# Merge, value products and output projection of the sample rows in the four column groups of TensorE

## What is computed

```python
def sample_attention(q_lat, q_pe, ckv_new, kr_new, cache_ckv, cache_kr, page_table):
    ...
    carry, _ = lax.scan(page_step, init, page_table.T)      # running max m, sum l, acc over the past rows
    sc_new = jnp.where(causal, scores(ckv_new, kr_new), NEG_INF)
    _, l, acc = update(carry, sc_new, ckv_new)
    o = acc / l[..., None]                                   # 8 sequences x 16 heads x 256 latents
    ...
def mla_out(o_lat, w_ukv, w_o):
    o = jnp.einsum("blhc,chd->blhd", o_lat, w_ukv[..., QK_NOPE:])     # 16 heads x 64
    return o.reshape(o.shape[0], o.shape[1], N_HEADS * V_HEAD) @ w_o  # 1024 x 1024
...
        x = x + ga1[:, None, :] * y
        h = modulate(rmsnorm(x, g_norm[layer, 1]), sh2, sc2)
        x = x + ga2[:, None, :] * peer(h, ...)
```

## Time and profile before

| | us |
|---|---|
| median of 3 runs (3669.32 to 3676.19) | 3672.77 |
| the profiled execution | 3665.84 |
| its span in the trace | 3664.0 |
| busy PE / DVE / ACT / POOL | 2650.3 / 2367.8 / 1223.5 / 1307.2 |
| expert gathers of layer 0 / layer 1, about | 454 to 1790 / 2304 to 3640 |
| attention between them, about | 1930 to 2262 |

### The profile page before, as it was taken

One profiled execution on the slowest core, in us unless ns is written; L12 is line 12 of the kernel. 1 busy time (PEld: TensorE's weight loads), 2 busy tenths in 40 slices (PEclk: granted clock), 3 DMA queues, 4 the chain that ended last, 5 costly groups with the idle time before them and its releaser, 6 DMA issues.

```text
span 3664.0 us, 63101 instructions
## 1 busy us (share of the span) xinstructions
PE 2650.3 (72%) x24936; PEld 987.7 (27%) x24936; DVE 2367.8 (65%) x5633; ACT 1223.5 (33%) x3811; POOL 1307.2 (36%) x1153
## 2 busy tenths in 40 slices
PE   4564899867766866658789996777686668666676
PEld 3353632403200400012225664322031004001100
DVE  8645387687776677555553541878867766765645
ACT  1212133434333333334432220343343343333333
POOL 5300033444444444433413510334444444443432
PEclk7666899867766966769999997777787679777667
DMA  8755599999999999999962044899999999999997
GB/s 330 209 140 200 220 396 411 405 419 410 409 420 419 409 420 420 403 420 381 393 218 107 19 187 157 322 400 403 421 402 417 421 419 409 421 420 400 417 420 319
DMA packets 214367, 1276.43 MB, mean 348 GB/s; under 512 B 54568, under 2 KB 60080, under 8 KB 67208
## 3 DMA queue, kind: packets, MB, share of 16 engines
q0 software_dynamic: 151552, 1109.46, 74.2%
q1 hardware_dynamic: 61968, 162.67, 12.8%
q10 hardware_dynamic: 576, 0.59, 0.1%
HBM read 1258.85 MB, written 11.43 MB: 347 GB/s over the span
## 4 chain that ended last, share of the span: by engine, by line
DMA 35%; PE 35%; DVE 19%; ACT 5%; issue 4%; SPq 1%; DVEq 1%; POOL 0%; PEldq 0%; ACTq 0%; POOLq 0%
DMA arena<-peer_uv,arena 34%; PE psum L2522 12%; DVE arena L1981 8%; PE psum L2469 6%; PE psum L2430 3%; DVE arena L1598 3%; PE psum L2870 2%; PE psum L2601 1%; PE psum L2670 1%; DVE arena L1607 1%; ACT arena L1339 1%; ACT arena L1336 1%; DVE arena L1892 1%; DVE arena L1992 1%; ACT arena L1326 1%
## 5 line engine op out<-in xcount | busy, mean ns | idle before, releaser
L2522 PE MATMUL psum<-arena 32*32 32x512 f32 x16384 | 1528.0, 819 | 740.3 <-ACT arena L1339 733.7
L1101 POOL DMA_INDIRECT arena<-peer_uv,arena x1040 | 1136.4, 1093 | 2007.5 <-PE psum L2522 1536.6
L1981 DVE SCALAR_TENSOR_TENSOR arena<-arena 128x1024 f32<-128x1024 f32 x1040 | 1273.6, 1226 | 743.5 <-DMA arena<-peer_uv,arena 731.7
L2522 PEld LDWEIGHTS psum<-arena 32*32 32x32 f32 x16384 | 216.5, 119 | 1915.0 <-ACT arena L1339 1813.8
L1326 ACT ACTIVATE arena<-arena 128x1 f32<-128x1 f32 x1040 | 210.3, 202 | 1533.3 <-DVE arena L1981 1532.2
L1339 ACT ACTIVATE arena<-arena 128x32 f32<-128x32 f32 x1024 | 329.0, 321 | 33.4
L1336 ACT ACTIVATE arena<-arena 128x1 f32<-128x1 f32 x1040 | 306.0, 294 | 33.8
L2469 PEld LDWEIGHTS psum<-arena 128*128 128x128 f32 x2048 | 245.7, 198 | 72.5 <-issue 69.5
L2469 PE MATMUL psum<-arena 128*128 128x128 f32 x2048 | 263.4, 286 | 2.2 <-ACT arena L1279 2.2
L2327 PE MATMUL psum<-arena 128*9 128x128 f32 x2048 | 98.8, 374 | 111.3 <-DMA arena<-b_mod 111.3
L1598 DVE TENSOR_TENSOR arena<-arena 128x512 f32<-128x512 f32 (+8 forms) x182 | 149.7, 823 | 18.7 <-ACT arena L1169 5.6
(11 more groups left out here) (293 smaller groups left out, 2379.5 us busy)
## 6 DMA issues: line engine op xcount, KB each, us to landing
arena<-w_mod SPq DMA_DIRECT2D x64, 1024.0 KB
arena<-peer_wq SPq DMA_DIRECT2D x12, 2048.0 KB, 12.6
arena<-peer_uv,arena POOLq DMA_INDIRECT x1040, 10.4
arena<-w_glu SPq DMA_DIRECT2D x5, 2048.0 KB, 12.8
arena<-mod_rows SPq DMA_DIRECT2D x4, 1024.0 KB
arena<-w_o SPq DMA_DIRECT2D x1, 4096.0 KB
arena<-x_after_layer SPq DMA_DIRECT2D x7, 512.0 KB
arena<-w_uq SPq DMA_DIRECT2D x1, 3072.0 KB, 15.0
```

The costliest lines, as they stand in the source:

```text
L1101: pool.indirect_dma_start(ring[r], None, a[f"peer_uv{t // 5}"], bass.IndirectOffsetOnAxis(ap=ix, axis=0)).then_inc(landed[r], 16)
L1981: dve.scalar_tensor_tensor(out=u, in0=u, scalar=1.0, in1=h, op0=ALU.mult, op1=ALU.mult, accum_out=at(DOTS + (t % 2) * 2 * P + m, 1)).then_ ...
L2522: ins = pe.matmul(acc_of(t, i, c), diag[rows, r, :], ring[r][rows, D + 512 * c:D + 512 * (c + 1)], start=(m == 0), stop=last, skip_group_c ...
```

## The change

The same results are computed with the work spread over the four column groups.

- `SW` has 32 columns for each sequence and lies where `SNEW` was. In the merge `SW` (32 columns) and `WNM` (16) are now stationary and `acc` and `KVR[0]` (256 latents) move; the sequences 4 r + g, g = 0 to 3, write the four groups of PSUM bank 2, once for r = 0 and once for r = 1. 16 matmuls. The result has heads on partitions and latents in columns, so DVE copies it (128 x 512), PE turns it (4 full turns), and DVE copies it in two parts to `olt`.
- The value products stay 32 matmuls of 64 columns, but heads 4 g + m write group g, so DVE copies 128 x 256 and PE turns 2 pieces.
- The projection writes quarter g of the 1024 outputs to group g: 32 matmuls of 256 columns (`sample_project`).
- Gate and residual rows of the sample are loaded in quarters, 256 columns on partitions 32 g to 32 g + 7, by four DMAs each instead of one; the store is four DMAs too, and the semaphore counts follow.

```diff
@@ program
-        SW = o; o += NB * NH
+        SW = SNEW
@@ attention_sync
-                sp.dma_start(at(MH + D, D, 0, NB), mod_dram[1:NC9, 8 * D:9 * D]).then_inc(s_mw, 16)
+                for g in range(4):
+                    sp.dma_start(at(MH + D, 256, 32 * g, 32 * g + NB),
+                                 mod_dram[1:NC9, 8 * D + 256 * g:8 * D + 256 * (g + 1)]).then_inc(s_mw, 16)
...
+                        for g in range(4):
+                            sp.dma_start(at(MX, 256, 32 * g, 32 * g + NB), x2s_dram[:, 256 * g:256 * (g + 1)]
+                                         ).then_inc(s_rld[0], 16)
@@ attention_store
+                for g in range(4):
+                    sp.dma_start(x3s_dram[:, 256 * g:256 * (g + 1)], at(MX, 256, 32 * g, 32 * g + NB)
+                                 ).then_inc(s_rst[0], 16)
@@ merge (DVE)
-                dve.tensor_tensor(at(SW, NB * NH).rearrange("p (b h) -> p b h", b=NB),
-                                  psum[:, 5, 0:NB].unsqueeze(2).to_broadcast([P, NB, NH]),
-                                  at(EYE, NH).unsqueeze(1).to_broadcast([P, NB, NH]), ALU.mult).then_inc(s_mg, 1)
+                dve.tensor_tensor(at(SW, NB * 32).rearrange("p (b h) -> p b h", b=NB),
+                                  psum[:, 1, 0:NB].unsqueeze(2).to_broadcast([P, NB, 32]),
+                                  eye32.unsqueeze(1).to_broadcast([P, NB, 32]), ALU.mult).then_inc(s_mg, 1)
                 dve.wait_ge(s_mg, 7)
-                dve.tensor_copy(olt, psum[:, 4, 0:2 * NB * NH].rearrange("p (c b h) -> p c h b", c=2, b=NB)
-                                ).then_inc(s_mg, 1)
+                dve.tensor_copy(at(OO, 512), psum[:, 2, :]).then_inc(s_mg, 1)
+                dve.wait_ge(s_mg, 9)
+                for c in range(2):
+                    ins = dve.tensor_copy(olt[:, c].rearrange("p h (r g) -> p h r g", r=2),
+                                          psum[:, 3, :].rearrange("p (r c g h) -> p c h r g", r=2, c=2, g=4)[:, c, 0:NH])
...
@@ attention_pe
-                for c in range(2):
-                    for b in range(NB):
-                        out = psum[:, 4, (c * NB + b) * NH:(c * NB + b + 1) * NH]
-                        pe.matmul(out, acc[:, b, P * c:P * (c + 1)], at(SW + b * NH, NH), start=True, stop=False)
-                        ins = pe.matmul(out, at(KVR[0] + P * c, P, 0, NB), at(WNM + b * NH, NH, 0, NB),
-                                        start=False, stop=True)
+                for r in range(2):
+                    for g in range(4):
+                        b = 4 * r + g
+                        pe.matmul(psum[32 * g:32 * g + 32, 2, KVL * r:KVL * (r + 1)], at(SW + b * 32, 32), acc[:, b, :],
+                                  start=True, stop=False, skip_group_check=True)
+                    for g in range(4):
+                        b = 4 * r + g
+                        ins = pe.matmul(psum[32 * g:32 * g + NH, 2, KVL * r:KVL * (r + 1)],
+                                        at(WNM + b * NH, NH, 0, NB), at(KVR[0], KVL, 0, NB), start=False, stop=True,
+                                        skip_group_check=True)
                 ins.then_inc(s_mg, 1)
                 pe.wait_ge(s_mg, 8)
-                for h in range(NH):
-                    for c in range(2):
-                        ins = pe.matmul(psum[0:NB, h // 8, VH * (h % 8):VH * (h % 8 + 1)], olt[:, c, h, :],
-                                        wv[:, c, VH * h:VH * (h + 1)], start=(c == 0), stop=(c == 1))
+                for j in range(4):
+                    ins = pe.transpose(psum[:, 3, P * j:P * (j + 1)], at(OO + P * j, P), ident)
+                ins.then_inc(s_mg, 1)
+                pe.wait_ge(s_mg, 10)
+                for m in range(4):
+                    for c in range(2):
+                        for g in range(4):
+                            h = 4 * g + m
+                            ins = pe.matmul(psum[32 * g:32 * g + NB, 0, VH * m:VH * (m + 1)], olt[:, c, h, :],
+                                            wv[:, c, VH * h:VH * (h + 1)], start=(c == 0), stop=(c == 1),
+                                            skip_group_check=True)
                 ins.then_inc(s_os, 1)
-                project(4)
+                sample_project()
@@
+            def sample_project():
+
+                pe.wait_ge(s_on, 1)
+                for j in range(2):
+                    ins = pe.transpose(psum[:, 1, P * j:P * (j + 1)], at(OO + 512 + P * j, P), ident)
+                ins.then_inc(s_ot, 1)
+                pe.wait_ge(s_otc, 9)
+                ot = at(OTT, D).rearrange("p (k t) -> p k t", k=KD)
+                for k in range(KD):
+                    for g in range(4):
+                        ins = pe.matmul(psum[32 * g:32 * g + NB, 2, 0:256], ot[:, k, 0:NB],
+                                        wo[:, k, 256 * g:256 * (g + 1)], start=(k == 0), stop=(k == KD - 1),
+                                        skip_group_check=True)
+                ins.then_inc(s_yy, 1)
```

More of the change, by code:

```diff
@@ L242, in row_no @@
                     if row_slot(q, m) == slot and not (passes is LOADS and (q, m) in NOT_LOADED)]
-            return 16 * len(mine)
+            return 16 * sum(4 if row == ("residual", 4) else 1 for row in mine)
         ROUNDS = ([("u", r) for r in range(NR)] + [("k", r) for r in range(NR)]
@@ L1560, in attention_act @@
                 act.wait_ge(s_ot, 1)
-                act.activation(at(OTT, D).rearrange("p (k t) -> p k t", k=KD)[:, :, 0:NB],
-                               psum[:, 6:8, :].rearrange("p b (k t) -> p (b k) t", k=4)[:, :, 0:NB], ACT.Copy
+                act.activation(at(OTT, D).rearrange("p (g j t) -> p j g t", g=4, j=2)[:, :, :, 0:NB],
+                               psum[:, 1, 0:256].rearrange("p (j g t) -> p j g t", j=2, g=4)[:, :, :, 0:NB], ACT.Copy
                                ).then_inc(s_otc, 1)
@@ L2240, in attention_dve @@
                 dve.wait_ge(s_os, 1)
[L2241 removed]
+                dve.tensor_copy(at(OO + 512, 256), psum[:, 0, 0:256]).then_inc(s_on, 1)
                 attention_out(4)
@@ L2272, in merge @@
                 dve.wait_ge(s_mg, 1)
-                nmt, lmt = psum[0:NB, 4, 0:P], psum[0:NB, 4, P:2 * P]
+                nmt, lmt = psum[0:NB, 0, 0:P], psum[0:NB, 0, P:2 * P]
                 link(dve.tensor_reduce(mn, nmt.rearrange("p (g h) -> p h g", g=4), AX.X, ALU.min))
@@ L2780, in attention_pe @@
                 pe.wait_ge(s_cnm, NB)
-                pe.transpose(psum[0:NB, 4, 0:P], at(NM, NB), ident)
-                pe.transpose(psum[0:NB, 4, P:2 * P], at(LSUM, NB), ident).then_inc(s_mg, 1)
+                pe.transpose(psum[0:NB, 0, 0:P], at(NM, NB), ident)
+                pe.transpose(psum[0:NB, 0, P:2 * P], at(LSUM, NB), ident).then_inc(s_mg, 1)
                 pe.wait_ge(s_mg, 4)
-                pe.transpose(psum[:, 5, 0:NB], at(EX, P, 0, NB), ident[0:NB, 0:NB]).then_inc(s_mg, 1)
+                pe.transpose(psum[:, 1, 0:NB], at(EX, P, 0, NB), ident[0:NB, 0:NB]).then_inc(s_mg, 1)
@@ L2853, in project @@
             def project(j):
-                R = rows5(j)
-                if j == 4:
-                    pe.wait_ge(s_on, 1)
-                    for k in range(KD):
-                        ins = pe.transpose(psum[:, 6 + k // 4, P * (k % 4):P * (k % 4) + R], at(OO + P * k, P, 0, R),
-                                           ident[0:R, 0:R])
-                    ins.then_inc(s_ot, 1)
-                elif j:
+                if j:
                     pe.wait_ge(s_x3, j)
-                y0 = 5 if j < 4 else 6
-                pe.wait_ge(s_otc, 2 * (j + 1) if j < 4 else 9)
-                pe.wait_ge(s_mw, 96 + 48)
+                pe.wait_ge(s_otc, 2 * (j + 1))
+                pe.wait_ge(s_mw, 96 + 96)
                 ot = at(OTT, D).rearrange("p (k t) -> p k t", k=KD)
@@ L2869, in project @@
                     for k in range(KD):
-                        ins = pe.matmul(psum[0:R, y0 + n_, :], ot[:, k, 0:R], wo[:, k, 512 * n_:512 * (n_ + 1)],
+                        ins = pe.matmul(psum[:, 5 + n_, :], ot[:, k, :], wo[:, k, 512 * n_:512 * (n_ + 1)],
                                         start=(k == 0), stop=(k == KD - 1))
+                ins.then_inc(s_yy, 1)
[11 more added lines that the diff above has]
+                                        skip_group_check=True)
                 ins.then_inc(s_yy, 1)
```

26 lines of the change are left out of this document (14 added, 12 removed).

## The result

| | before | changed |
|---|---|---|
| median, us (4 runs each) | 3671.05 | 3639.64 |
| span of the profiled execution | 3664.0 | 3645.6 |
| first merge product to the first load of layer 1 | 46.43 | 18.83 |
| first merge product to the first expert gather | 87.03 | 59.74 |

The ratio is 0.992, with a 95% interval of 0.9898 to 0.9942. Forecast was 3644.5 in a range of 3636 to 3656, faster by 0.8%; measured is 3639.64, faster by 0.9% in the medians. The changed kernel was timed again beside the experiments: 3646.04 against 3672.00, ratio 0.9923 (0.9903 to 0.9943). The two differences of medians, 31.4 and 26.0, lie on either side of what the traces show for the chain: 27.6 us to the first load, 27.3 to the first gather.

What follows compares the result with a forecast made beforehand. The sample rows' lone serial chain between the expert stages was taken as the bound; its terms summed to 18.2 us against 46.4, 28.2 less, so the median 3672.77 became 3644.5, range 3636 to 3656.

Steps and rivals of the forecast that it cites:

- What bounds the kernel: Between layer 0's and layer 1's expert stages, sample attention runs alone for 46.43 us; each microsecond cut comes off the time.
- the third rival: Layer 1's expert stage gives the time back: 520 gathers on average 0.054 us longer cancel the saving (3672.8); chance 0.05.
- The pricing of grouped products: Priced from the cache values' 32 records in 3.41 to 3.52 us: four groups really run at once.
- The second rival: The column groups do not run at once after all: 3669.7 (no change) or 3681.8 (slower); chance 0.03.
- The first rival: Matmuls with 8 or 16 output columns overlap less, adding 2.7 us to the PE terms: 3647.2; chance 0.06.
- wider product: DVE product ahead of the merge, 128x256 for 128x128: 0.42 us for 0.29, so +0.13.
- merge: 16 matmuls of 256 columns, four at once at 1.2 GHz: 3.5 us, lower bound 1.9, before 17.28.
- four turns: New full-width transposes after the merge: 0.70 us, bounds 0.66 and 1.4 if the clock is low.
- value products: 32 matmuls of 64 columns, bounded by the spacing of 64 records: 2.0 us, bounds 1.2 and 3.6, before 6.37.
- two turns: Two full transposes for eight narrow ones ahead of the output projection: 0.5 us, between 0.35 and 0.70.
- projection: Output projection, 64 records four at once, half in 3.4 us, the rest at full clock in 1.8: 5.3 us, before 15.73.
- store: Four quarter-row issues 0.38 us apart, and the landing: 2.93 us, bounds 1.79 and 7.2, before 1.79.

Runs made afterwards that it cites:

- the projection in one group: Changed kernel with the output projection's 32 matmuls of 256 columns all writing partitions 0 to 7 instead of four groups; 3666.63 us (1 run).
- the exchanged order: Changed kernel with the merge's eight matmuls of 32 output columns first and the eight of 16 columns behind them; 3641.77 us (1 run).

## Why the prediction was right

**What bounds the kernel** was right, and carried it: a chain with one engine at work at a time passes each microsecond on. The stretch shrank by 27.6 us, the first gather by 27.3, the two differences of medians are 31.4 and 26.0. The experiments bear it out together: in the seven measurements of four or five runs each the first gather moved by 14.0, 16.2, 27.3, 27.5, 32.8, 34.3 and 36.4 us, and their ratios, times the median of before, say 13, 15, 29, 28, 35, 33 and 36, each with an interval of 5 to 8 us to either side. (In the trace the links of the chain are a little looser than the text's 0.07 us: 0.13 ahead of the gate product, 0.08 ahead of the store. Nothing hangs on it.) Layer 1's stage did not give it back: from the first gather to the end it is 2.1 and 3.6 us longer in the two profiles of the changed kernel, where the third rival needed 28, and 0.7 shorter to 4.0 longer in the others without an order. Whether 2 us of it belong to the change one profile of before can't tell.

**The pricing of grouped products** was right: 4 at once, for 16 and for 8 output columns too. The second rival fell by the projection in one group (15.41 against 5.41). For the merge no run separates the groups from the exchange of its operands; at 0.43 us a record its 32 records in one group would take 13.7 us (an estimate), so of the 13.2 us saved some 9.6 would be the groups' and the rest the exchange. The first rival, less overlap in narrow groups, fell too: the projection's first 3.4 us at the low clock hold 36 records, and four at once at 0.107 us each would be 32 and the four that start together. The Trainium skill (TensorE: Matmul & The Clock Gate, Measured speedup vs the span model) gives 2.38 times for three groups. This case's records disagree with the efficiency of 0.79 that follows from it: at the same low clock four records take the 0.43 us of one. The whole projection gained less, 2.85 times, since the shorter one spends more of its time at the low clock.

**Term by term** (forecast, measured in the first profile): wider product +0.13, +0.13; merge 3.5, 4.12; copy 0.74, 0.75; four turns 0.70, 1.15; two copies 0.65, 0.68; value products 2.0, 1.96; copy 0.48, 0.48; two turns 0.5, 0.72; ACT 0.28, 0.28; projection 5.3, 5.41; DVE 0.97, 0.96; store 2.93, 2.32. Three were mis-sized.
- *Merge, 0.6 low*, and above the 3.5 that also stood as its high end. The text argued from the step to a full-width turn, where it saw no gap, that a change of shape costs nothing. That row misled: over it (2209.46 to 2212.87) the mean clock was 0.53 and not 0.50, so the 32 records were done early and the gap was hidden. At the full clock the trace of before shows it:

```profile
2196.18 1.06 PE L2848 MATMUL psum<-arena 128*32 128x128 f32 x32
2197.16 2.40 PE L2831 MATMUL psum<-arena 128*128 128x128 f32 x20
```

From the grouped records to the full-width ones it is 0.98 us, where the columns make 0.85: 0.13 for the change. Between the merge's shapes, 32 columns with 128 rows and 16 with 8, it is 0.14 us, three times, as the exchanged order shows. The last wave's tail is 0.27 us (2227.00 to 2228.12 is 1.12, the columns 0.85), the tail that the text itself had for the key scores. The Trainium skill (TensorEngine Tiling (Array Packing), Key Properties) has a drain at such a change; a cost is there, but it is a third of the 0.43 us at which the text priced it, and that it is a drain no row shows.
- *Turns, 0.7 low together.* I took the 0.70 from a row at full clock though I had the clock at 1.2 GHz for the step ahead. The bound of 1.4 covered the four turns; the two, at 0.72, lie just above their bound of 0.70.
- *Store, 0.6 high.* The four issues stand 0.34 us apart and not 0.38, and the last lands 1.30 us after its issue begins, not 1.78. That a small quarter lands sooner than the whole row was not in the sum. It is so in all profiles (1.79 us in the two with one store, 2.32 or 2.33 in the six with four whose end the first load waits for); the cause is open.

Against the forecast they are +0.6, +0.7 and -0.6, so the store hides one of the other two: the chain came out at 18.96 us for 18.2, and the saving at 27.5 for 28.2. That the time (3639.64, then 3646.04) lies on either side of the 3644.5 is no finer test: it scatters by more than this 0.7. The projection's 5.3 was right by its mechanism (3.4 us at the low clock, then full), yet its size depends on where the clock rises: 5.15 to 5.62 us in five profiles, 6.10 to 6.43 in the three whose merge was the old one or had the extra matmuls ahead of it. For the value products the size was right, but its reason is open: at 1.2 GHz the columns themselves (64 records of a quarter of 0.107) make 1.7 us as well as the spacing of records does, and no run had this step at the full clock.

## What to carry to other kernels

Small products of few output rows that sit alone on a chain are worth grouping; price them from a grouped row of the same kernel at the clock that the stretch has, and every neighbouring step at that clock too. Test parts one by one, but expect their gains not to add where the clock level is shared between them. When a serial chain has been cut, look at what still waits behind its last store: here a smaller buffer for the result let loads start that the larger one, by the layout, forbade.

## What the runs showed of the hardware

- A change of shape with work ready behind it costs 0.13 to 0.16 us on PE between the merge's two grouped shapes at 1.2 GHz and 0.12 to 0.14 at 2.4, and 0.13 from a grouped shape to full width at 2.4.
- Four column groups run at once: at 1.2 GHz four records of 256 columns take 0.43 us, as one does in one group.
- Extra matmuls in a wait of PE kept the clock at 1.00 for the 2.4 us of the merge; 0.8 us after its end it was at 0.50, and the projection was slower by 0.8 us.
- 1.6 MB of modulation rows, one row spread to 128 partitions, landed in 7.7 and 7.9 us with no other load behind it and in 8.2 with 4.5 MB behind it. While it moved with nothing behind it, it ran at 319 to 362 GB/s (the gathers reach 411), but over the whole wait it is only about 210.
- With a matmul of `start=True` for the other half of a PSUM bank placed between two that accumulate in the first half, on the same partitions, the result was wrong (relative error 0.61); in the order of the diff it is right.
